# Gates and two projections of a hybrid mixer computed by tokens, with 512 weight columns in each matmul

## What is computed

```python
def hybrid_mixer(h, w_in, ..., w_proj_attn, w_proj_ssd, w_out):
    proj = h @ w_in
    (q, k, v, qi, ki, wi, z, xbc, dt_raw, g_attn, g_ssd) = jnp.split(proj, offsets, axis=-1)
    ...
    a = dsa_attention(q, k, v, qi, ki, wi)                 # (1, 256, 1024)
    b = mamba2_branch(z, xbc, dt_raw, ...)                 # (1, 256, 2048)
    merged = jax.nn.sigmoid(g_attn) * (a @ w_proj_attn) + jax.nn.sigmoid(g_ssd) * (b @ w_proj_ssd)
    return merged @ w_out
```

## Time and profile before

| | |
|---|---|
| median of three runs | 1805.31 us (1805.21 to 1806.47) |
| the profiled execution | 1806.57 us, of it the span 1804.8 us |
| mean granted clock | 0.989 |
| PE busy | 1729.4 us (96%), 13858 matmuls and as many weight loads |
| DVE busy | 1335.7 us (74%) |
| ACT busy | 1019.2 us (56%) |
| POOL busy | 677.2 us (38%) |
| chain that ended last | PE 81%, DVE 8%, ACT 6% |
| DMA | 288.42 MB, 160 GB/s mean |

### The profile page before, as it was taken

How to read it: one execution, slowest core, us unless ns; L and a number is a source line. 1 busy time by engine, 2 the same in 40 slices (tenths; PEclk the granted TensorE clock), 3 DMA queues, 4 the chain that set the end, 5 groups by cost and what they waited for, 6 DMA issues and landing times.

```text
span 1804.8 us, 33652 instructions
## 1 busy us (share of the span) xinstructions
PE 1729.4 (96%) x13858; PEld 1684.1 (93%) x13858; DVE 1335.7 (74%) x1967; ACT 1019.2 (56%) x1571; POOL 677.2 (38%) x417
## 2 busy tenths in 40 slices
PE   6989999997999999999999999999999998999997
PEld 6989999986999999999889999999999888999997
DVE  5758875575686859974779589778986578769794
ACT  5465555663654564576663566546467565366462
POOL 6641104951310265344454501038244355331113
PEclk9989999998999999999999999999999999999999
DMA  7435645641455554463234455555355333545552
GB/s 268 151 110 183 199 164 173 200 118 35 149 187 184 168 191 152 158 204 130 99 124 164 164 174 191 180 181 181 123 187 170 111 118 132 176 153 195 187 174 84
DMA packets 80649, 288.42 MB, mean 160 GB/s; under 512 B 9072, under 2 KB 9328, under 8 KB 80368
## 3 DMA queue, kind: packets, MB, share of 16 engines
q1 hardware_dynamic: 79488, 283.15, 47.1%
q10 hardware_dynamic: 1008, 3.11, 0.5%
HBM read 285.18 MB, written 1.05 MB: 159 GB/s over the span
## 4 chain that ended last, share of the span: by engine, by line
PE 81%; DVE 8%; ACT 6%; issue 3%; POOL 1%; DMA 0%; SPq 0%; ACTq 0%; DVEq 0%; POOLq 0%
PE lin L682 25%; PE lin L684 25%; PE lin L683 25%; ACT w_hi L1164 2%; DVE arena L2163 1%; DVE sq L2104 1%; PE stat L755 1%; ACT sq L1538 1%; PE logit L1004 1%; PE tr L858 1%; PE tr L1082 1%; PE lin L983 1%; ACT L1538 1%; DVE std L2160 1%; PE logit L941 1%
## 5 line engine op out<-in xcount | busy, mean ns | idle before, releaser
L1164 ACT ACTIVATE w_hi<-w_raw 128x1024 fp32r<-128x1024 f32 (+1 forms) x546 | 537.1, 1032 | 291.9 <-PE lin L684 291.0
L477 POOL TENSOR_TENSOR w_lo<-w_raw,w_hi 128x1024 fp32r<-128x1024 f32 (+1 forms) x198 | 476.4, 2417 | 358.6 <-ACT w_hi L1164 249.7
L682 PE MATMUL lin<-h_hi,w_hi 128*128 128x256 f32 x1952 | 560.5, 287 | 24.5 <-DVE w_lo L477 16.6
L682 PE MATMUL lin<-hid_hi,w_hi 128*128 128x256 f32 x1936 | 553.6, 286 | 10.8 <-DVE hid_lo L486 7.2
L683 PE MATMUL lin<-h_lo,w_hi 128*128 128x256 f32 x1952 | 555.0, 284 | 0.0
L684 PE MATMUL lin<-h_hi,w_lo 128*128 128x256 f32 x1952 | 554.9, 284 | 0.0
L684 PE MATMUL lin<-hid_hi,w_lo 128*128 128x256 f32 x1936 | 548.7, 283 | 0.0
L683 PE MATMUL lin<-hid_lo,w_hi 128*128 128x256 f32 x1936 | 548.6, 283 | 0.0
L477 DVE TENSOR_TENSOR w_lo<-w_raw,w_hi 128x1024 fp32r<-128x1024 f32 (+1 forms) x348 | 482.9, 1392 | 37.7 <-ACT w_hi L1164 36.8
L682 PEld LDWEIGHTS lin<-h_hi,w_hi 128*128 128x128 f32 x1952 | 377.5, 193 | 26.6 <-issue 20.6
L682 PEld LDWEIGHTS lin<-hid_hi,w_hi 128*128 128x128 f32 x1936 | 372.3, 192 | 13.8 <-DVE hid_lo L486 6.1
(11 more groups left out here) (307 smaller groups left out, 2129.3 us busy)
## 6 DMA issues: line engine op xcount, KB each, us to landing
w_raw<-in_upA SPq DMA_DIRECT2D x112, 512.0 KB, 3.7
w_raw<-in_upB SPq DMA_DIRECT2D x64, 512.0 KB, 4.1
w_raw<-in_xbc SPq DMA_DIRECT2D x48, 512.0 KB, 4.1
w_raw<-in_dnA SPq DMA_DIRECT2D x32, 512.0 KB, 3.6
w_raw<-in_dnB SPq DMA_DIRECT2D x32, 512.0 KB, 3.5
w_raw<-in_z SPq DMA_DIRECT2D x32, 512.0 KB, 4.1
w_raw<-in_gates SPq DMA_DIRECT2D x32, 512.0 KB, 3.9
w_raw<-in_ps SPq DMA_DIRECT2D x32, 512.0 KB, 3.9
```

The source lines that it names most:

```text
L477: eng.tensor_tensor(w_lo[slab.slot][:, half, part], w_raw[slab.slot][:, half, part], w_hi[slab.slot][:, half, part].bitcast(F32), ALU.subt ...
L682: nc.tensor.matmul(out, lhs[0], rhs[0], start=first, stop=False)
L1164: nc.scalar.activation(w_hi[slab.slot][:, half, part], w_raw[slab.slot][:, half, part], ACT.Copy)\
```

## The change

The stages gates, pa and ps of both layers are computed by tokens. The activations are now stationary (128 tokens of one chunk) and the weights stream past them, 512 outputs wide. A slab now holds 512 input channels by 512 outputs (`wide_slabs`), and `wide_products` makes 24 matmuls of it: four chunks, two blocks of tokens, three passes. Two slabs (gates, pa) or four (ps) together fill a pair of banks, one for each block of tokens; both are waited for ahead of the pair. `merged` and the gates are stored by token.

- ACT takes the Sigmoids of a finished pair after slabs 2, 4 and 6, and the last pair after the first two squares of the norm.
- DVE multiplies the results of pa in pairs after slabs 1 and 3, and those of ps after slabs 5 and 7 (`merge`).
- out wants `merged` by channel. PE transposes it (`merged_transposes`, 16 transposes of 128x128 into `tr`, `stat` and `logit`): the first half after ps slab 6, the second after the first four chunks of out slabs 0 and 1, which are now both begun before either ends. ACT and DVE round and split from there.
- Slab ps n asks for `bn_lo` of one group: ps 0 group 0, ps 1 group 1, ps 2 group 0, ps 3 group 1.

The number of slabs, their bytes, roundings and splits stay as they were.

```diff
@@ -433,8 +435,8 @@
         xtok = [[arena[:, at * T:(at + 2) * T] for at in tile_at] for tile_at in ((12, 14, 8, 10), (57, 59, 61, 63))]
-        gates = arena[:, 17 * T:33 * T].rearrange("p (m g t) -> p m g t", g=2, t=T)
-        merged = cut(57, 8)
+        gates = arena[:, 17 * T:33 * T].rearrange("p (u n) -> p u n", n=WIDE)
+        merged = arena[:, 57 * T:65 * T].rearrange("p (t n) -> p t n", t=2)
         ix_sc, ix_w = cut(65, 1), cut(66, 2)
@@ -464,6 +466,16 @@
                 body(slab_at(stage, n, l), n, n % RING)
+        def wide_bank(stage, n, t, l):
+            return slab_at(stage, n - n % 2 + t, l)
+        def wide(bank):
+            return lin[bank][:, :, :].rearrange("p a t -> p (a t)")
+        merged_in = [tr[:, :].rearrange("p (c t) -> p c t", t=T), stat[:, :].rearrange("p (c t) -> p c t", t=T),
+                     logit[:, 0:2, :], logit[:, 2:4, :]]
@@ -738,6 +750,30 @@
                 mm.then_inc(s.lin_done, 2)
+            def wide_products(stage, n, l, tokens, first=True, last=True, wait_chunk=None):
+                slab = slab_at(stage, n, l)
+                for half in range(2):
+                    slab.wait_split(pe, half)
+                    for i in range(2):
+                        chunk = tokens[2 * half + i]
+                        if wait_chunk is not None:
+                            wait_chunk(2 * half + i)
+                        cols = slice(i * WIDE, (i + 1) * WIDE)
+                        w = w_hi[slab.slot][:, half, cols], w_lo[slab.slot][:, half, cols]
+                        for t in range(2):
+                            lhs = tuple(part[:, t * P:t * P + P] for part in chunk)
+                            mm = passes(wide(wide_bank(stage, n, t, l).bank), lhs, w,
+                                        first and half == 0 and i == 0, last and half == 1 and i == 1)
+                    mm.then_inc(s.lin_done, 1)
+            def wide_pair(stage, n, l, operand):
+                if n % 2 == 0:
+                    for t in range(2):
+                        wide_bank(stage, n, t, l).wait_bank_free(pe)
+                wide_products(stage, n, l, operand[n % 2 * 4:n % 2 * 4 + 4], n % 2 == 0, n % 2 == 1)
@@ -1117,7 +1153,7 @@
                     if c % 2 == 0:
-                        slab_products(slab_at("gates", c // 2, l), operand)
+                        wide_pair("gates", c // 2, l, operand)
                     if c == 0:
@@ -1131,20 +1167,45 @@
                 for g in range(SG):
...
+                    wide_pair("pa", g, l, raw)
                     pe.wait_ge(s.bn_pre, SG * l + g + 1)
                     for k in range(2):
                         mm = nc.tensor.matmul((tr, stat)[g % 2][:, 0:T], const("mean512"),
                                               sq[:, 4 * (g % 2) + k, :], start=(k == 0), stop=(k == 1))
                     mm.then_inc(s.bn_sum, 1)
+                def merged_transposes(i):
+                    pe.wait_ge(s.merged_tok, 4 * l + 2 * i + 2)
+                    for b in (2 * i, 2 * i + 1):
+                        for c in range(2):
+                            for t in range(2):
+                                at = (2 * b + c) * P
+                                mm = nc.tensor.transpose(merged_in[b][:, c, t * P:t * P + P], merged[:, t, at:at + P], ident)
+                        mm.then_inc(s.merged_tr, 1)
                 for n in range(8):
+                    if n in (0, 2):
+                        for t in range(2):
+                            wide_bank("ps", n, t, l).wait_bank_free(pe)
+                    k = n // 4 * 2 + n % 2
+                    wide_products("ps", n, l, (operand, raw)[n // 4][n % 2 * 4:n % 2 * 4 + 4], k == 0, k == 3,
+                                  lambda _i: pe.wait_ge(s.bn_lo, SG * l + k + 1))
+                    if n == 6:
+                        merged_transposes(0)
+                out, merged_op = [slab_at("out", j, l) for j in range(4)], hid_op(2 + l, MERGED)
+                def wait_merged(c):
+                    pe.wait_ge(s.merged_lo, 4 * l + c // 2 + 1)
+                for slab in out[0:2]:
+                    slab.wait_bank_free(pe)
+                    for half in range(2):
+                        slab.wait_split(pe, half)
+                    late_part(slab, merged_op, range(NC4), DC - 1, wait_merged)
+                merged_transposes(1)
+                for slab in out[0:2]:
+                    late_part(slab, merged_op, range(NC4, DC), DC - 1, wait_merged)
+                closing(out[2:4], merged_op, None)
                 ffn(None, 5 + 2 * l, l)
@@ -1528,8 +1589,7 @@
                     slab = slab_at("gates", n, l)
-                    nc.scalar.activation(gates[:, n, :, :], lin[slab.bank][:, :, :], ACT.Sigmoid)\
-                        .then_inc(s.bank_free[slab.bank], 1)
+                    nc.scalar.activation(gates[:, n, :], wide(slab.bank), ACT.Sigmoid).then_inc(s.bank_free[slab.bank], 1)
@@ -1537,8 +1597,8 @@
                     done(slab_at("gates", m, l))
-                    if m % 2 == 1:
-                        for n in range(max(0, m - 2), m):
+                    if m % 2 == 0 and m:
+                        for n in (m - 2, m - 1):
                             gate_sig(n)
@@ -1553,6 +1613,7 @@
                 bn_square(1)
+                gate_sig(XCH // 2 - 2)
                 gate_sig(XCH // 2 - 1)
@@ -1568,17 +1629,17 @@
...
+                def merge_round(b):
+                    act.wait_ge(s.merged_tr, 4 * l + b + 1)
+                    nc.scalar.activation(hid_parts(2 + l, MERGED[2 * b], 2)[0], merged_in[b], ACT.Copy).then_inc(s.merged_hi, 1)
+                for n in range(8):
+                    if n == 7:
+                        merge_round(0)
+                        merge_round(1)
+                    done(slab_at("ps", n, l))
+                merge_round(2)
+                merge_round(3)
                 residual("out", 5 + 2 * l, lambda c: pcol2(l, "ffn_g", c), l)
@@ -2145,8 +2206,11 @@
                     slab.wait_done(dve)
-                    tt(merged[:, 2 * n:2 * n + 2, :], lin[slab.bank][:, :, :], gates[:, 2 * n:2 * n + 2, 0, :], ALU.mult)\
-                        .then_inc(s.bank_free[slab.bank], 1)
+                    if n % 2:
+                        part = slice(n // 2 * WIDE, (n // 2 + 1) * WIDE)
+                        for t in range(2):
+                            bank = wide_bank("pa", n, t, l).bank
+                            tt(merged[:, t, part], wide(bank), gates[:, n - 1 + t, :], ALU.mult).then_inc(s.bank_free[bank], 1)
@@ -2168,29 +2232,34 @@
...
+                def merged_rest(b):
+                    dve.wait_ge(s.merged_hi, 4 * l + b + 1)
+                    hi, lo = hid_parts(2 + l, MERGED[2 * b], 2)
+                    lo_part(nc.vector, lo, merged_in[b], hi).then_inc(s.merged_lo, 1)
+                def merge(i):
+                    part = slice(i * WIDE, (i + 1) * WIDE)
+                    gated = [acc[:, t, :, :].rearrange("p c n -> p (c n)") for t in range(2)]
+                    slab_at("ps", 5 + 2 * i, l).wait_done(dve)
+                    if i or l:
+                        dve.wait_ge(s.merged_tok, 4 * l + 2 * i)
+                    for t in range(2):
+                        bank = wide_bank("ps", 2 * i, t, l).bank
+                        tt(gated[t], wide(bank), gates[:, 4 + 2 * i + t, :], ALU.mult).then_inc(s.bank_free[bank], 2)
+                    for t in range(2):
+                        wide_bank("ps", 4 + 2 * i, t, l).wait_released(dve)
+                        tt(merged[:, t, part], merged[:, t, part], gated[t], ALU.add).then_inc(s.merged_tok, 1)
+                for n in range(6):
+                    weights(slab_at("ps", n, l))
+                merge(0)
+                weights(slab_at("ps", 6, l))
+                merged_rest(0)
+                merged_rest(1)
+                weights(slab_at("ps", 7, l))
+                merge(1)
+                merged_rest(2)
                 merged_rest(3)
@@ -2285,6 +2354,19 @@
     return [np.concatenate(chunks[2 * j:2 * j + 2]) for j in range(n // 4)]
+def wide_slabs(w, halves):
+    out = []
+    rows = w.shape[0] // halves
+    for p in range(halves):
+        for first in range(0, w.shape[1], WIDE):
+            for k in range(0, rows, 4 * P):
+                at = p * rows + k
+                block = w[at:at + 4 * P, first:first + WIDE].reshape(2, 2, P, WIDE)
+                out.append(block.transpose(2, 0, 1, 3).reshape(P, 2, HALF))
+    return np.stack(out)
@@ -2347,9 +2429,9 @@
         stages["z"].append(slab_of(w, pairs(XCH, at[6])))
-        stages["gates"].append(slab_of(w, [pair(m, m, at[9], at[10]) for m in range(DC)]))
-        stages["pa"].append(slab_of(i["w_proj_attn_2"][l], pairs(DC)))
-        stages["ps"].append(down_slabs(i["w_proj_ssd_2"][l], ((0, 8), (8, 8))))
+        stages["gates"].append(wide_slabs(w[:, at[9]:], 1))
+        stages["pa"].append(wide_slabs(i["w_proj_attn_2"][l], 1))
```

(1 more changed line is left out.)

43 lines of the change are left out of this document (3 added, 40 removed).

## The result

| | before | changed |
|---|---|---|
| median, runs of both side by side | 1806.82 us | 1809.41 us (1806.15 to 1813.05) |
| ratio | | 1.0015, 95% interval 1.0008 to 1.0021 |
| the profiled execution | 1806.57 us, of it the span 1804.8 us | 1809.44 us, of it the span 1807.7 us |
| mean granted clock | 0.989 | 0.986 |

The change costs 2.7 us (1.4 to 3.8, by the ratio). The forecast was 1.0 more than before, 1806.3, in a range of 1799.5 to 1812, with 0.2%, 3.6 us, as the least that would count as a change. The measured time lies in that range and the difference under that limit. But the small sum is the difference of larger terms, and three of them were wrong, in both directions.

The account below looks back on a forecast made before the run. A DVE and ACT loop bounds gates, then the norm chain, PE only late in ps. Per layer -0.9 through ps and +1.4 in merge and out give +0.5, +1.0 for both: 1806.3 us against 1805.31, range 1799.5 to 1812.

Parts of the forecast that it names:

- gates stage, moved Sigmoid rounds: Gates stage: Sigmoid rounds in mid-group cost 3.7 us, the old places 2.4, so 1.3 longer a layer (bounds 0.3 and 2.5).
- Sigmoids behind the squares: Norm chain: both last Sigmoids and their table load now stand between squares and rounding, 1.8 us more a layer.
- first reciprocal to the norm, without drops: From the norm chain's reciprocal through pa, ps, out and feed-forward to the norm: 2.6 us less a layer.
- drop behind the wait at ps: After PE's wait in ps: half clock costs 1.5 us a layer as before, since the new wait is nearly as long.
- the forecast's own signs: Right: matmuls 0.215 apart, gates stage 72 to 74.5 us, reciprocal near 945; wrong: 0.227 or 0.24, no PE wait at ps 2.
- What bounds it: Gates: a DVE and ACT loop, PE following; then the norm chain; PE's rate counts only from there to the end of ps.
- rival (a): Whole kernel: PE's busy time bounds, so 40 slabs each save 0.60 us, 24 us less, 1781; chance 0.04.
- PE's rate: Gates, pa, ps: a 512-column matmul takes 0.215 us with its weight load hidden, so a slab takes 5.16, 0.60 less.
- rival (b): Where PE bounds: 512-column matmuls cost 0.227 us, overhead added, 1.6 more a layer, 1809.5, slower; chance 0.18.
- The clock: Half clock follows the new ps 2 wait as it did the old one, 1.5 us a layer; no gates-stage drops priced.
- Waits in ps and out: PE waits three times between pa 3 and mid ps 2, last 3.6 us for DVE's split; about 1.2 after the last transposes.
- (c): No clock drop after shorter waits (1.5 us a layer), fewer POOL collisions in the chain (1 to 2): about 1800.5; chance 0.11.
- (d): Chain meets more POOL operations, or a layer's three PE waits drop the clock twice: 2 to 3 us a layer, about 1811; chance 0.07.

Follow-up runs that it names:

- b_sig_new: Kernel before, matmuls still 256 wide, with the gates' Sigmoid rounds moved to where the changed kernel has them; ratio 1.0044 to the kernel before.
- a_gates256: Changed kernel with the gates stage's 512-wide matmuls issued as two of 256 columns, except first and last of each accumulation; ratio 1.0018 to the kernel before.
- a_sig_old: Changed kernel with the gates' Sigmoid rounds put back where the kernel before had them; ratio 0.9994 to the kernel before.
- best_early_pool: Changed kernel with old Sigmoid places, last round ahead of slab 7's roundings, and POOL splitting ps 2's second half; 1793.35 us, ratio 0.9925 to the kernel before.
- a_lengths: Changed kernel plus unread matmuls of 128 to 512 columns behind its last layer; 0.111, 0.120, 0.173 and 0.227 us from start to start.
- a_fill: Changed kernel plus 12 unread matmuls ahead of each product of chunks 7, 11 and 15 in the gates stage; ratio 1.0003 to the kernel before.
- a_sig_early: Changed kernel with old Sigmoid places, but the last round in the stage ahead of slab 7's weight roundings; ratio 0.9969 to the kernel before.
- b_fill: Kernel before plus 28 unread matmuls inside PE's 3.92 us wait at the first ps slab; ratio 0.9979 to the kernel before.

## Why the prediction was right, point by point

| term, a layer | forecast | measured |
|---|---|---|
| gates stage, moved Sigmoid rounds | +1.3 | +1.1 (73.26 against 72.13, without drops) |
| Sigmoids behind the squares | +1.8 | +1.9 (b_sig_new +1.86, changed +1.93) |
| first reciprocal to the norm, without drops | -2.6 | -1.6 (95.36 against 96.96) |
| drop behind the wait at ps | 0 (stays) | -1.5 (gone) |
| drops in the gates stage | 0 (none) | +2.9 in layer 0, +1.4 in layer 1 |
| sum | +0.5 | +2.9 and +1.4 |

The total came out near the forecast partly by luck. Per layer, the piece from the first reciprocal on was 1.0 dearer than forecast and the new drops 2.9 and 1.4, while the old drop, carried over by the forecast, gave 1.5 back; and the drop between the mixers, which no term spoke of and which only the kernel before has in its profile, took another 1.4 off the difference of the two spans. Of the forecast's own signs, three came out against it: the start to start of 0.227, named as a sign of being wrong; a gates stage of 76.4 and 74.9, where 72 to 74.5 was to be right; and PE's waits for the mask product, 7.7 us in six instead of eight that "sum to some 10 us or more". The first reciprocal came at 948.29, not near 945.

- **What bounds it.** Right. The rate of PE counts for next to nothing in the gates stage (half a microsecond in a_gates256, nothing in a_sig_old), and the loop of DVE and ACT sets it (a_sig_old restores it to 0.01 us). 24 us from the shorter slabs, rival (a), was never to be had. The reckoning from one Sigmoid round and the spacing of the mask products gave +1.3, and the run without drops +1.1.
- **PE's rate.** Wrong. The step took 0.215 for 512 columns and gave the excess at 256 to the weight load. The excess of 0.013 is there at 256, 384 and 512 alike. The two loads 0.12 apart and a matmul rate of 0.12 were a coincidence taken for a cause: 128 columns run at 0.112, so no floor of 0.12 stands under them. The f32 rows of L1082, 0.43 for what the forecast took as two passes of 512 columns, did not carry over: an fp32r matmul of 512 columns takes 0.227, not half of 0.43. The Trainium skill ("TensorE: Matmul & The Clock Gate", section "Back-to-back issue gap") has 2.5 ns over the columns for an isolated matmul and 131 ns at 512 columns in a stream; this case's rows show 13 and 227, and they decide. The bound "0.227, if the 0.013 over 0.107 is added to each matmul whatever its length", on which rival (b) stood, is exact. It puts 1.6 a layer on the forecast. The changed kernel's own third piece, at full clock, is 95.15 where the forecast without the drop comes to 94.4 (98.40 - 2.6 - 1.4), so 0.8 off; 0.6 came back in the chain, which took 33.3 from the first reciprocal to the split of ps 2 (948.29 to some 981.6), not 33.9, and 0.2 in the wait behind the last transposes. That the chain is shorter when it starts later is not the width's doing: in b_sig_new, with narrow matmuls, it takes 21.66 from the first reciprocal to the end of PE's wait at ps 0, and 22.58 before. The forecast took it as it was, with 3 us either way; which operations no longer meet was not traced.
- **The clock.** Wrong in place. The forecast carried the old drop over to the new wait at ps 2 since the waits were alike. It went, and others came in the gates stage. There the forecast saw that PE's waits for L2112 would grow "by the same" as the slabs shrank, and that each mask product behind a Sigmoid round would come late, and put the longer waits of PE at nothing. It is the late round that lengthens them enough: with wide matmuls and the old places (a_sig_old) the longest is 1.04 and the stage has no drop, with narrow ones and the new places (b_sig_new) they are 1.7 to 2.2 and it has. The step that failed is this one: a wait of an engine off the path was priced at nothing. PE is off the path in this stage only at full clock; at half clock its product and scores come late for DVE.
- **Waits in ps and out.** Right in kind, place and order: three waits behind pa, the last for DVE's split (3.6 forecast, 2.83 measured), 0.98 behind the last transposes (1.2 forecast).
- **Rivals.** (b)'s rate came true. Its time, 1809.5, is the measured 1809.41 by luck: it was +4.2 on the 1805.31 known then, and the kernel before, measured beside the changed one, is at 1806.82, so +2.7 is what it has to be held against. The route was another too: its 1.6 a layer was given back, by the chain and by the old drop, and the drops in the gates stage filled the place. The "slower" that it gave did not come, by the limit of 3.6 us that the forecast had set, nor does its "decides from 0.217 on" follow from its sum: 264 matmuls reach the 3.6 us on top of the forecast's 1.0 only at 0.225. (c) "The clock does not drop after the shorter waits" was true for ps and outweighed elsewhere. (d), waits that drop the clock twice, named the mechanism but looked for it in ps.

## What to carry to other kernels

Measure a matmul's fixed part at two lengths before splitting it into "load" and "overhead"; one length cannot tell them apart. When an edit lengthens waits of TensorE, even off the critical path, look at the clock column of the stretches and try the cheapest test, which is to fill the wait with matmuls that nobody reads; it also gives the price of every drop. Compare the unchanged parts of two profiles first, since a drop that comes in one and not in the other can move the time as much as a small change does (1.4 us here). And when operands are regrouped so that a step needs two buffers at once, search what releases the second: here one Sigmoid held the second bank. From the changed kernel to best_early_pool, by moved Sigmoids and one moved weight split, it is 16.3 us by the ratios, while 512 columns instead of 256 are worth 4.5 to 5.2 us in that kernel. Whether the kernel before would gain from an earlier Sigmoid round too was not tried.

## What the runs showed of the hardware

- fp32r matmuls from 256 to 512 columns are columns / 2.4 GHz plus 0.013 us apart, on the same or alternating stationary tiles; at 128 columns 0.112 (a_lengths, one run). Every matmul has its weight load in the records, also when the tile stays the same (144 of each).
- In these stages half clock came for 3.4 us at a time, each time behind a wait of TensorE of 1.7 us or more, and matmuls put into the wait kept it away. The wait's length does not decide alone: at ps 2, 2.83 us (changed kernel) and 2.86 (a_fill) had no drop behind them, 2.84 (a_sig_old) and 2.87 (a_sig_early) had one; the same 1.98 had one in layer 1 and none in layer 0 (a_sig_old); the same 2.48 between the mixers had one in seven of twelve profiles. What else decides stays open.
- The price of such a stretch ran from nothing (second piece) to 1.5 us (b_fill) and 1.6 (second piece of a_sig_old, layer 1).
